# A fused two-block network: the attention's input product accumulated over pairs of feature blocks, and 32 modulation pieces computed on TensorE

## The reference

```python
shift, scale, gate = ada_modulation(c, ada_w[i, 0], ada_b[i, 0])
# silu(c) (1 x 1024) times a 1024 x 3072 matrix, plus a bias, cut in three
z = x * (1.0 + scale) + shift          # 256 tokens x 1024 features
# qkv = z @ attn_w_in (1024 x 1536: 8 query heads, 2 key heads, 2 value heads of 128)
# rotary embedding on the first 32 dimensions of each query and key head
# windowed softmax attention with a sink per head, then @ attn_w_out
x = layer_norm(DN_ALPHA * x + (1.0 + gate) * y, ln_g[i, 0], ln_b[i, 0])
```

## Time and profile before

| | us |
|---|---|
| median of 3 runs | 1612.23 (1610.78 to 1612.74) |
| the profiled execution's own time | 1610.23 |
| its span | 1608.9 |
| TensorE busy | 1359.3 (84%) |
| TensorE weight loads busy | 1175.1 (73%) |
| VectorE busy | 1124.6 (70%) |
| ScalarE busy | 698.6 (43%) |
| GpSimd busy | 62.3 (4%) |
| DMA | 311.89 MB, mean 194 GB/s |
| first matmul starts | 43.22 |
| first scores start | 89.99 |
| product with `attn_w_out` starts, ends | 139.42, 167.33 |

### The profile page before, as it was taken

One profiled execution on the slowest core, in us unless ns is written; L12 is line 12 of the kernel. 1 busy time (PEld: TensorE's weight loads), 2 busy tenths in 40 slices (PEclk: granted clock), 3 DMA queues, 4 the chain that ended last, 5 costly groups with the idle time before them and its releaser, 6 DMA issues.

```text
span 1608.9 us, 20642 instructions
## 1 busy us (share of the span) xinstructions
PE 1359.3 (84%) x7720; PEld 1175.1 (73%) x7720; DVE 1124.6 (70%) x1509; ACT 698.6 (43%) x887; POOL 62.3 (4%) x54
## 2 busy tenths in 40 slices
PE   0867699997999977998974998765769999999996
PEld 0756599996777756998973787654667777777874
DVE  6656677776677666777786647885566767767675
ACT  2331344441665762444442433210225656656553
POOL 2100100001000001000000000231000000000000
PEclk9989899999999978999997998987769999999998
DMA  9426677773566646655660345200024887879662
GB/s 365 144 98 242 204 262 262 290 289 115 196 245 213 209 157 239 250 209 221 222 215 8 130 158 197 66 1 3 9 104 145 282 305 246 292 252 330 232 239 110
DMA packets 84068, 311.89 MB, mean 194 GB/s; under 512 B 9344, under 2 KB 9568, under 8 KB 83360
## 3 DMA queue, kind: packets, MB, share of 16 engines
q1 hardware_dynamic: 82080, 298.88, 52.3%
q10 hardware_dynamic: 1888, 11.69, 2.2%
HBM read 309.48 MB, written 1.05 MB: 193 GB/s over the span
## 4 chain that ended last, share of the span: by engine, by line
PE 65%; DVE 23%; ACT 5%; DMA 4%; issue 2%; POOL 0%; SPq 0%; DVEq 0%; ACTq 0%; POOLq 0%
PE ps L406 64%; DVE w_low L365 5%; DVE junk L365 4%; DMA ring<-moe 2%; ACT w_high L365 2%; DMA ring<-stream 2%; DVE t_one L365 1%; DVE t_two L365 1%; DVE rs L365 1%; DVE x L365 1%; DVE qp L365 1%; DVE pf L365 1%; DVE r_two L365 1%; DVE sc L365 1%; ACT h_high L365 1%
## 5 line engine op out<-in xcount | busy, mean ns | idle before, releaser
L365 DVE TENSOR_TENSOR w_low<-ring,w_high 128x1024 fp32r<-128x1024 f32 x356 | 437.0, 1228 | 174.3 <-ACT w_high L365 150.1
L365 ACT ACTIVATE w_high<-ring 128x1024 fp32r<-128x1024 f32 x356 | 377.6, 1061 | 317.5 <-PE ps L406 175.5
L406 PE MATMUL ps<-x_high,w_high 128*128 128x256 f32 (+1 forms) x784 | 236.3, 301 | 80.3 <-DVE x_low L365 71.5
L406 PE MATMUL ps<-x_low,w_high 128*128 128x256 f32 (+1 forms) x784 | 233.4, 298 | 0.0
L406 PE MATMUL ps<-x_high,w_low 128*128 128x256 f32 (+1 forms) x784 | 233.3, 298 | 0.0
L406 PEld LDWEIGHTS ps<-x_high,w_high 128*128 128x128 f32 x784 | 154.9, 198 | 92.0 <-issue 85.7
L365 DVE CUSTOM_DVE_ANT_0 junk<-ring,cond 128x1024 f32<-128x1024 f32 x125 | 155.5, 1244 | 23.4 <-DMA ring<-stream 8.3
L406 PEld LDWEIGHTS ps<-x_low,w_high 128*128 128x128 f32 x784 | 155.0, 198 | 2.6
L406 PEld LDWEIGHTS ps<-x_high,w_low 128*128 128x128 f32 x784 | 154.6, 197 | 2.8
L406 PE MATMUL ps<-h_high,w_high 128*128 128x256 f32 x512 | 145.9, 285 | 3.6 <-DVE w_low L365 2.0
L406 PE MATMUL ps<-h_low,w_high 128*128 128x256 f32 x512 | 145.0, 283 | 0.0
(11 more groups left out here) (299 smaller groups left out, 2094.3 us busy)
## 6 DMA issues: line engine op xcount, KB each, us to landing
ring<-stream SPq DMA_DIRECT2D x376, 512.0 KB, 4.7
ring<-moe SPq DMA_DIRECT2D x192, 512.0 KB, 4.6
tab_two<-tab ACTq DMA_DIRECT2D x1, 2824.0 KB, 15.4
gw<-gw ACTq DMA_DIRECT2D x1, 2304.0 KB, 14.0
cond<-cvec ACTq DMA_DIRECT2D x3, 512.0 KB, 6.8
x<-xT ACTq DMA_DIRECT2D x1, 1024.0 KB, 11.9
ctx<-ctxT ACTq DMA_DIRECT2D x1, 1024.0 KB, 4.8
pos<-posT ACTq DMA_DIRECT2D x1, 1024.0 KB, 7.6
```

Of the source, the lines that this page charges most:

```text
L365: return op(*a, **k).then_inc(self.sem, 1)
L406: return pe.matmul(out, stationary, moving, start=start, stop=stop, skip_group_check=True)
```

## The change

Part 1, the modulation pieces. The first 32 pieces (kind "e", 16 chunks of two) are transposed on the host: inputs on the partitions, outputs along the free dimension. TensorE multiplies each with silu(c) as a column (C8, 128 x 8, a load of 4 KB of its own): 8 float32 matmuls per piece, stationary 128 x 128 from the ring, moving 128 x 1 (`ada_piece`). The result is a column of PSUM. VectorE's and GpSimd's work on those 32 pieces goes.

Part 2, pairs of feature blocks. The pieces come as shift and scale of two feature blocks (4 pieces a pair), and `attn_w_in` as 3 pieces per pair: A (4 query tiles), B (4 query tiles), C (2 key tiles and the values). All 10 tiles and the values keep their sums in PSUM banks 0 to 5 over the four pairs. VectorE modulates a pair as soon as its 4 pieces are summed in bank 6 or 7. Copies to QK and rotations come in the last pair alone, key heads first.

Part 3, attention. Pieces 16 to 31 are put between the scores, transposes and value products on TensorE (`modulate`). Three rotations precede the first scores on VectorE, two follow.

Part 4, moved work. X times ALPHA goes from GpSimd to ScalarE (after the second batch), the recurrence's constants from the start to beside the product with `attn_w_out`, and the loads of RPAR and of the two conditions to behind the copies to QK.

```diff
-POOL_PIECES = (1, 6, 11)
+ADA_ORDER = [0, 4, 1, 5, 2, 6, 3, 7] + list(range(8, 48))
+ADA_COL = [2 * j for j in ADA_ORDER] + [96 + 2 * j for j in A2_ORDER]
+E_CHUNKS = 16
+QKV_PARTS = ("ABC", "ABC", "ABC", "CAB")
+QKV_AT = {(p, part): 3 * p + n for p, parts in enumerate(QKV_PARTS) for n, part in enumerate(parts)}
+ROPE = (4, 0, 1, 2, 3)
...
-    order = pieces("a" * 8 + "w" * 6 + "a" * 8 + "wa" * 4 + mlp)
+    order = "e" * 8 + "www" + "eeee" + "www" + "eeee" + "w" * 6 + "e" * 16 + pieces("wa" * 4 + mlp)
...
+    def ada_piece(n, out):
+        c = ADA_AT[n]
+        pe.wait_ge(arrived[c % RING], 16 * (c // RING + 1))
+        for k in range(KT):
+            ins = mm(out, m.piece(c)[:, k * P:(k + 1) * P], m.C8[:, k:k + 1], k == 0, k == KT - 1)
+        ins.then_inc(s.ada_pe, 1)
+    def first_modulation(p, js=range(4)):
+        if p >= 2:
+            pe.wait_ge(s.t2, p - 1)
+        for j in js:
+            ada_piece(4 * p + j, PS[:, 6 + p % 2, j:j + 1])
...
+    def heads(p, part, tiles):
+        w = QKV_AT[p, part]
+        pe.wait_ge(s.w_low, split_upto(w + 1))
+        pe.wait_ge(s.x_low, p + 1)
+        for tile in tiles:
+            for k in range(2):
+                lo = k * 512 + (tile - 4 * "ABC".index(part)) * P
+                ins = mm3(PS[:, tile // 2, (tile % 2) * 256:(tile % 2 + 1) * 256], weight(w, lo), pair(XIN, slice(None), 2 * p + k),
+                          p == 0 and k == 0 and tile % 2 == 0, p == 3 and k == 1)
+            if p == 3 and tile in (9, 1, 5):
+                ins.then_inc(s.qk_mm, 1)
...
+    def rotate(r):
+        n2 = ROPE[r]
...
+    PV_BANK = (0, 1, 3, 0)
+    beside = iter(range(2 * E_CHUNKS - 16))
+    def modulate(n):
+        for _ in range(n):
+            j = next(beside)
+            ada_piece(16 + j, PS[:, 2, j:j + 1])
...
+        modulate(1)
...
+    pe.wait_ge(s.silu_c8, 1)
+    first_modulation(0)
+    first_modulation(1)
+    for part in QKV_PARTS[0]:
+        columns(0, part)
+    first_modulation(2)
+    columns(1, "A")
+    first_modulation(3, (0, 1))
+    columns(1, "B")
+    first_modulation(3, (2, 3))
+    columns(1, "C")
+    for part in QKV_PARTS[2]:
+        columns(2, part)
+    pe.wait_ge(s.t2, 4)
+    pe.wait_ge(s.ones, 1)
+    columns(3, "C")
+    heads(3, "A", (0, 1))
+    rotate(0)
+    heads(3, "A", (2, 3)).then_inc(s.used, 1)
+    rotate(1)
+    heads(3, "B", (4, 5))
+    rotate(2)
+    heads(3, "B", (6, 7)).then_inc(s.used, 1)
+    rotate(3)
     scores(0)
+    rotate(4)
+    modulate(2)
+    scores(1)
+    modulate(3)
     for n in range(4):
-        if n < 3:
+        if 1 <= n < 3:
             scores(n + 1)
+            modulate(3)
         attend(n)
+    modulate(1)
...
-    act.dma_start(m.RPAR, rpar).then_inc(s.in_rnn, 16)
-    act.dma_start(m.CB[:, 0, :], cvec[0:1, :].broadcast_to([P, D])).then_inc(s.in_c, 16)
+    act.dma_start(m.C8, ccol).then_inc(s.in_c8, 16)
+    act.dma_start(m.X, xT).then_inc(s.in_x, 16)
     act.dma_start(m.PAR, par).then_inc(s.in_par, 16)
-    act.dma_start(m.X, xT).then_inc(s.in_x, 16)
-    act.wait_ge(s.lam_abs, 1)
-    A(m.lam_t[1], m.lam_t[1], ACT.Exp, s.lam_exp)
-    act.wait_ge(s.in_c, 16)
-    A(m.CB[:, 0, :], m.CB[:, 0, :], ACT.Silu, s.silu_c)
-    act.dma_start(m.TAB, tab).then_inc(s.in_att, 16)
-    act.dma_start(m.ident, ident_d).then_inc(s.in_att, 16)
-    act.dma_start(m.CB[:, 1, :], cvec[1:2, :].broadcast_to([P, D])).then_inc(s.in_c2, 16)
-    for n, piece in enumerate(POOL_PIECES):
-        half = m.ada_halves[n % 2]
-        act.wait_ge(s.ada_pool, n + 1)
-        A(half, half, ACT.Copy, s.ada_half, accum_out=m.MOD[:, piece:piece + 1])
-    act.wait_ge(s.in_par, 16)
+    act.wait_ge(s.in_c8, 16)
+    A(m.C8, m.C8, ACT.Silu, s.silu_c8)
...
-    modulated(MOD_FIRST)
-    high_upto(4)
-    for n2 in range(5):
-        high_upto(min(W_QKV + 2 * n2 + 5, W_ATT))
-        act.wait_ge(s.used, W_QKV + 2 * n2 + 2)
-        A(m.QK[:, 2 * n2:2 * n2 + 2, :], PS[:, n2 % 2, :].rearrange("p (n t) -> p n t", n=2), ACT.Copy, s.qk_out)
+    high_x(0)
+    high_x(1)
+    act.dma_start(m.TAB, tab).then_inc(s.in_att, 16)
+    act.dma_start(m.ident, ident_d).then_inc(s.in_att, 16)
+    high_upto(W_QKV + 3)
+    high_x(2)
+    high_upto(W_QKV + 6)
+    high_x(3)
     high_upto(W_ATT)
-    act.wait_ge(s.in_c2, 16)
-    A(m.CB[:, 1, :], m.CB[:, 1, :], ACT.Silu, s.silu_c2)
-    act.wait_ge(s.used, W_ATT)
-    A(m.VT, PS[:, 0:2, 0:256], ACT.Copy, s.v_out)
+    act.wait_ge(s.in_par, 16)
...
+            A(m.lam_t[1], m.lam_t[1], ACT.Exp, s.lam_exp)
+        if n == 1:
+            for h in range(2):
+                A(m.X[:, 4 * h:4 * h + 4, :], m.X[:, 4 * h:4 * h + 4, :], ACT.Copy, s.x_alpha, scale=ALPHA)
...
-    pool.wait_ge(s.silu_c, 1)
-    for n, c in enumerate(POOL_PIECES):
-        pool.wait_ge(arrived[c % RING], 16 * (c // RING + 1))
-        if n >= 2:
-            pool.wait_ge(s.ada_half, n - 1)
-        op(pool.tensor_tensor, m.ada_halves[n % 2], m.piece(c), m.CB[:, 0, :], ALU.mult, inc=s.ada_pool)
-    pool.wait_ge(s.in_x, 16)
-    pool.wait_ge(s.x_low, x_splits(MOD_FIRST) + 4)
-    for k in range(0, KT, 2):
-        op(pool.tensor_scalar, m.X[:, k:k + 2, :], m.X[:, k:k + 2, :], ALPHA, None, ALU.mult, inc=s.x_next)
...
-    for j in range(8):
-        modulation(m.junk, only=[n for n in range(2) if 2 * j + n not in POOL_PIECES])
-    vv.wait_ge(s.ada_half, len(POOL_PIECES))
-    bias(0, 16, "ada_b", 0)
-    op(vv.tensor_scalar, m.combo[:, 0:8], m.MOD[:, 8:16], 1.0, None, ALU.add)
+    more = m.combo[:, 48:56]
+    op(vv.tensor_scalar, more, m.par("ada_b", 8, 8), 1.0, None, ALU.add)
     vv.wait_ge(s.in_x, 16)
-    lows = modulated(MOD_FIRST, m.X, m.combo[:, 0:8], m.MOD[:, 0:8])
-    low_upto(1)
-    lows()
+    def first_modulation(p):
+        two = slice(2 * p, 2 * p + 2)
+        vv.wait_ge(s.ada_pe, 4 * p + 4)
+        op(vv.tensor_tensor, m.MOD[:, two], PS[:, 6 + p % 2, 0:2], m.par("ada_b", 2 * p, 2), ALU.add)
+        op(vv.tensor_tensor, m.combo[:, two], PS[:, 6 + p % 2, 2:4], more[:, two], ALU.add)
+        for k in (2 * p, 2 * p + 1):
+            op(vv.tensor_scalar, m.T2[:, k, :], m.X[:, k, :], m.combo[:, k:k + 1], m.MOD[:, k:k + 1], ALU.mult, ALU.add, inc=s.t2 if k % 2 else None)
+        low_part(MOD_FIRST, p, 0)
+    first_modulation(0)
+    first_modulation(1)
+    low_upto(W_QKV + 3)
+    first_modulation(2)
+    low_upto(W_QKV + 6)
+    first_modulation(3)
+    low_upto(W_ATT)
...
-        for _ in range(2):
-            modulation(m.junk)
-    bias(16, 8, "ada_b", 16)
+    vv.wait_ge(s.ada_pe, 2 * E_CHUNKS)
+    op(vv.tensor_tensor, m.MOD[:, 16:32], PS[:, 2, 0:16], m.par("ada_b", 16, 16), ALU.add)
     op(vv.tensor_scalar, m.gate1, m.MOD[:, 16:24], 1.0, None, ALU.add)
-    vv.wait_ge(s.x_next, 4)
+    vv.wait_ge(s.x_alpha, 2)
+    vv.wait_ge(s.silu_c, 1)
...
-    attn_in = np.concatenate([out_tiles(wi[:, 0:1280]), v_in])
+    wi = wi.reshape(4, 2, P, 3, 512).transpose(0, 3, 2, 1, 4).reshape(4, 3, P, HALF)
+    attn_in = np.stack([wi[p, "ABC".index(part)] for p, parts in enumerate(QKV_PARTS) for part in parts])
...
+    adas[:2 * E_CHUNKS] = [piece.reshape(P, KT, P).transpose(2, 1, 0).reshape(P, HALF) for piece in adas[:2 * E_CHUNKS]]
```

More of the change, by code:

```diff
@@ L108, in stream_order @@
     assert len(order) == 2 * N_CHUNKS
-    out, n = [], {"w": 0, "a": 0, "p": 0}
-    for piece in range(2 * N_CHUNKS):
-        kind = "p" if piece in POOL_PIECES else order[piece]
+    out, n = [], {"w": 0, "a": 0, "e": 0}
+    for kind in order:
         out.append((kind, n[kind]))
@@ L164 @@
 Sems = collections.namedtuple("Sems", """
-    x_pos in_rnn in_c in_par in_x in_att in_c2 in_cc in_gw in_late in_filt in_sel out
-    w_high w_low used ada ada_pool ada_half
+    x_pos in_rnn in_c in_c8 in_par in_x in_att in_c2 in_cc in_gw in_late in_filt in_sel out
+    w_high w_low used ada ada_pe x_alpha
     act dve pool
-    lam_abs lam_exp silu_c silu_c2 silu_cc ones
+    lam_abs lam_exp silu_c8 silu_c silu_c2 silu_cc ones
     t2 x_high x_low x_add x_next
-    qk_out rope_mm rope_ps qk v_out score_mm sc smax exp prob pt_mm pt pv_mm ot
+    qk_mm qk_out rope_mm rope_ps qk v_out score_mm sc smax exp prob pt_mm pt pv_mm ot
     mean_mm xc sq var_mm root
@@ L225, in __init__ @@
         self.junk_rnn = view("junk_rnn", aXL, 1024)
-        self.ada_halves = [view("ada_half", aT1 + 1024 * j, 1024) for j in range(2)]
+        self.C8 = view("cond_cols", aX + 4096 - 8, 8)
         a0 = aB + 1056
@@ L458, in tensor_program @@
[L458 to L466, removed]
-    batches = ((0, 0), (0, 1), (1, 0), (1, 1))
+    def ada_piece(n, out):
[4 more added lines that the diff above has]
+        ins.then_inc(s.ada_pe, 1)
@@ new lines, in values, with columns @@
+    def values(p):
+        w = QKV_AT[p, "C"]
+        for b in range(2):
+            for k in range(2):
+                ins = mm3(PS[:, 5, b * 256:(b + 1) * 256], pair(XIN, slice(None), 2 * p + k, slice(b * P, (b + 1) * P)), weight(w, k * 512 + 256, 256),
```

(49 more changed lines are left out.)

110 lines of the change are left out of this document (55 added, 55 removed).

## The result

The changed kernel takes 1643.44 us (median, 1642.6 to 1647.28) against 1611.51 us of the kernel before in the same runs (1605.2 to 1612.74): ratio 1.0212, 95% interval 1.0196 to 1.0228. It is slower by about 32 us, clear of the spread of the runs. The profiled execution has a span of 1641.1 us against 1608.9.

The account below looks back on a forecast made before the run. Loads and VectorE's modulation bound the first 43 us, then TensorE, then attention with VectorE between scores and transposes. The sum: 1610.2 + 11.3 up to the scores + 13.5 in attention = 1635.0 us; range 1610 to 1663.

Parts of the forecast that it names:

- the likeliest case: Whole kernel: the prediction's own forecast, 1635.0 us, range of its own 1625 to 1648, chance 0.48.
- two new waits of over 4 us: TensorE ahead of the first and second pair: waits for VectorE's w_low behind the next modulation, 4.5 and 4.4 us.
- The price of a piece: TensorE, 16 instructions per piece: 3.42 us at the lower clock (0.214 each), 1.72 at the higher (0.107).
- The prediction's inference from 16 columns to one: Pieces on TensorE: one moving column costs what 16 or 4 do, since the weight load sets the pace.
- The case that pieces raise the clock themselves: Pieces on TensorE, third rival: first 8 take 16.7 us, scores 5.9 us earlier, whole 1604.9; chance 0.10.
- the first 5 us at the higher clock: Pieces behind real matmuls: clock falls 5 us after them, so 4 pieces take 8.8 us, three in attention 5.3.
- the second rival: Clock lower than taken: 14 us more ahead of the scores, 29 in attention; 1678, half of it 1656; chance 0.17.
- The new wait of 1.5 us ahead of the third pair: Third pair needs w_high and w_low behind the fourth modulation, ready at 80.3 us, 4.4 after 75.9.
- A rotation: TensorE, third and fourth pair: four rotations of 0.94 us each, 3.8 in all.
- About 5.5 us lay on the chain: Attention: of the 16 pieces removed from VectorE, about 5.5 us stood on the chain (four from 127.31).
- Behind it: nothing: After attention: recurrence's constants beside the attn_w_out product cost nothing, up to 4 us if late; later parts unchanged.
- the other signs: Marks of being right, such as DMA share well under 1 in the first 40 us and attention above 60 us.

Follow-up runs that it names:

- the first run with 128 columns: Changed kernel with silu(c)'s column streamed 128 times for pieces 0 to 15, 32 times for pieces 16 to 31; 1617.97 us, ratio 1.0073.
- the run with one matmul of eight: Changed kernel with only the first of eight matmuls of each of pieces 16 to 31; 1631.01 us, ratio 1.0142.

## Why the prediction was right, and where it was off

The forecast was 1635.0 us, the measured median 1643.4, inside the range and inside the range of the likeliest case. The mechanism is the forecast one: pieces at the lower clock's price, two new waits of over 4 us, TensorE as the bound of attention. The size is partly luck: the product with attn_w_out moved by 35.6 us where the sum has 24.8, and of the 10.8 us missed 3.4 came back behind it, where the sum has nothing. Step by step, in us:

| step | predicted | measured |
|---|---|---|
| start of TensorE | 5.0 | 4.7 |
| 8 pieces | 27.4 | 27.5 |
| wait behind them | 4.5 | 4.6 |
| first pair | 11.1 | 10.1 |
| 4 pieces | 8.8 | 10.7 |
| wait behind them | 4.4 | 4.4 |
| second pair and 4 pieces, to the third pair | 19.1 | 22.8 |
| third and fourth pair with rotations | 21.0 | 21.8 |
| first scores at | 101.3 | 106.6 |
| attention | 62.9 | 68.5 |

- The price of a piece held exactly: 0.214 and 0.107 per instruction. The prediction's inference from 16 columns to one is shown by the trace, and its cause by the runs with more columns. The Trainium skill, "TensorE: Matmul & The Clock Gate", section "LDWEIGHTS (loading the stationary operand)", gives a load as its columns over 1.2 GHz, 107 ns for 128 of them. Here that is the price at the higher clock alone; at the lower one the traces show twice that, 0.214 us.
- The case that pieces raise the clock themselves is refuted: 27.5 us of them without a gap stay at 0.214. The same loads under 128 moving columns ran at 0.11 us each from 9 us on (the first run with 128 columns). The Trainium skill says in the same page, Part 1, section "What's actually happening", that activity releases the throttle; here 27.5 us of these loads with one column did not.
- The term that was mis-sized is how long the clock stays high behind real matmuls: "the first 5 us at the higher clock". That came from a gap. Behind the first pair it fell after about 3.3 us (PEclk 0.77 in 48 to 52), behind the first scores and their rotation after about 2.1 (0.95 in 108 to 112), only behind the fourth scores after about 5. The shorter time makes the 4 pieces 10.7 instead of 8.8, the two and three pieces of attention 5.1, 7.1, 7.8 and 5.5 instead of 3.4 and three times 5.3, and the scores 3.76 and 2.87 instead of 2.0. It was in the second rival, of whose 43 us about a quarter came true (5.3 of 14 ahead of the scores, 5.6 of 29 in attention). The other way, the clock rose 3.1 us after the start of the first pair, not after 5.85, which makes that pair 10.1 instead of 11.1. The new wait of 1.5 us ahead of the third pair didn't come, because the 24 matmuls ahead of it ran at the lower clock, took 4.9 us and covered it; with 128 columns, where they took less, it came with 1.57.
- A rotation costs TensorE 1.16 us instead of 0.94: from one to the next are 2.60 us, of which the 12 matmuls between are 1.44.
- "About 5.5 us lay on the chain" for VectorE's pieces was wrong, though the sum does not use it: with them gone (the run with one matmul of eight) the last transposes come 0.6 us earlier relative to the value product ahead of them. Another path was nearly as long.
- "Behind it: nothing" was off, and by the prediction's own sign: it calls a part behind the product with attn_w_out that moves by more than 2 us a mark of being wrong. The shift against the kernel before is 35.6 us at that product, 37.1 at the first product of the MLP, 36.3 at its second, 33.6 at the second block's output product and 32.2 at the end. The profiles of the variants, from the start of that product to the end, lie between 4.1 us less and 1.4 us more than the kernel before, and single runs of the kernel before lie up to 7.5 us apart, so the cause stays open.
- Of the other signs, the DMA share was well under 1 only from 16 us on (0.38 to 0.77 in the stretches of 4 us up to 40); from 4 to 16 us it was 0.97 to 1.02.

What bounds what, then: the idea of pairs is worth 17 us ahead of the scores if pieces are nearly free. It is turned into a loss by two things, each undone alone and both together: the clock, which stays or falls low when TensorE is kept busy with the loads of single columns (35 us, from 1643.4 to 1608.0; 33 when each is taken against its own runs of the kernel before), and the order of w_low (11 us alone, or 9 by that measure and 10.0 at the scores; 15.5 with the clock kept).

## What to carry to other kernels

A matrix times one vector on TensorE costs its weight loads, here 0.107 us for every 128 x 128 half of a float32 product, and twice that when the clock is low, which such work itself brings about: price it at the lower clock, for the real matmuls behind it too. If it has to be there, stream the vector's column many times over; under the load it is free, and here 128 times kept the clock where 32 did not. And when a stage is cut into pieces that are handed from engine to engine, put each helper's work for the current piece ahead of its work for the next: it is the order on the helper, not its load, that left TensorE waiting.

## What the runs showed of the hardware that was not expected

- The clock falls under a busy engine: TensorE busy 4.00 of 4.00 us in 52 to 56 with PEclk 0.50. The prediction took this over from a gap; not expected was how soon it falls, 2.1 to 5.2 us behind the real matmuls.
- More moving columns made the kernel faster: 25 us with 128 and 32 columns, 35 us with 128 nearly everywhere, with the same number of instructions.
- After 4.6 us without matmuls the first pair started at the lower clock even where the pieces ahead had run at the higher one (0.72 mean in 24 to 30 us with 128 columns), so the gaps cost their length and a slow start: with 128 columns everywhere, closing them brought the scores 16.6 us forward (90.81 to 74.25), of which the gaps themselves are about 10.6.
